# Expert tokens fetched by indirect DMA from a DRAM copy, the residual rows as accumulator, the gate row multiplied in on POOL

## What is computed

```
x = x + gate1 * m                                     # attention half, before the change's place
h = rms_norm(x, g_ffn) * (1.0 + scale2) + shift2
# expert_choice_ffn, for each set (512 latent tokens: cap 64; 128 context tokens: cap 16)
aff = softmax(h @ w_router)                           # 16 experts
gates, idx = top_k(swapaxes(aff, 1, 2), cap)          # each expert picks its cap tokens
xe = h[idx]
ye = (silu(xe @ w_gate) * (xe @ w_up)) @ w_down * gates
x = x + gate2 * zeros.at[idx].add(ye)                 # gate2: one row of 1024 for each set
y = rms_norm(x, g_final)
```

## Time and profile before

| | us |
|---|---|
| median of 3 runs | 1370.84 (1369.69 to 1372.06) |
| profiled execution | 1370.9 |
| its span in the profile | 1368.9 |
| PE / DVE / ACT / POOL busy | 1227.7 / 970.9 / 751.7 / 135.6 |
| first matmul of the first expert group | 702.55 |
| last matmul of the last expert's down product starts | 1323.79 |

### The profile page before, as it was taken

How to read it: one execution, slowest core, us unless ns; L and a number is a source line. 1 busy time by engine, 2 the same in 40 slices (tenths; PEclk the granted TensorE clock), 3 DMA queues, 4 the chain that set the end, 5 groups by cost and what they waited for, 6 DMA issues and landing times.

```text
span 1368.9 us, 17500 instructions
## 1 busy us (share of the span) xinstructions
PE 1227.7 (90%) x6001; PEld 969.7 (71%) x6001; DVE 970.9 (71%) x1245; ACT 751.7 (55%) x1049; POOL 135.6 (10%) x210
## 2 busy tenths in 40 slices
PE   2789987897879999999489999999999999999972
PEld 0568766676767777777378888788887888778851
DVE  1743527788847143244779999999999999799956
ACT  1522225666743212222658887688776887578831
POOL 2131430000000000010440001000010000100002
PEclk9899998999999999999789999999999999999986
DMA  9632221101052543554549997899888997999911
GB/s 325 268 140 64 91 69 39 40 21 40 0 201 75 186 123 124 215 202 154 192 153 383 372 365 243 301 385 369 336 271 286 385 364 271 369 340 379 371 40 77
DMA packets 109481, 295.26 MB, mean 216 GB/s; under 512 B 29857, under 2 KB 31602, under 8 KB 108642
## 3 DMA queue, kind: packets, MB, share of 16 engines
q1 hardware_dynamic: 102802, 265.99, 53.8%
q0 software_dynamic: 6032, 19.43, 4.4%
q10 hardware_dynamic: 576, 8.91, 1.7%
HBM read 276.78 MB, written 12.27 MB: 211 GB/s over the span
## 4 chain that ended last, share of the span: by engine, by line
PE 77%; DVE 11%; DMA 4%; ACT 3%; issue 3%; POOL 1%; SPq 1%; DVEq 0%; ACTq 0%; POOLq 0%
PE ps L1080 12%; PE ps L1081 12%; PE ps L1082 12%; PE ps L671 9%; PE ps L672 9%; PE ps L673 9%; PE ps L849 2%; PE ps L865 2%; DMA raw<-in_w_mod_dram 2%; DVE neg_max L1685 2%; DVE raw_lo L1775 2%; DMA raw<-in_w_exp_up_dram 1%; PE ps L888 1%; PE ps L693 1%; PE ps L1051 1%
## 5 line engine op out<-in xcount | busy, mean ns | idle before, releaser
L1775 DVE TENSOR_TENSOR raw_lo<-raw,w_hi 128x1024 fp32r<-128x1024 f32 x256 | 300.8, 1217 | 33.7 <-ACT w_hi L1421 27.0
L1421 ACT ACTIVATE w_hi<-raw 128x1024 fp32r<-128x1024 f32 x252 | 259.1, 1057 | 62.4 <-PE ps L1082 58.4
L1080 PE MATMUL ps<-w_hi,xe_hi 128*128 128x512 f32 x512 | 207.4, 405 | 1.8 <-DVE xe_lo L1949 1.8
L1082 PE MATMUL ps<-w_hi,xe_lo 128*128 128x512 f32 x512 | 201.7, 394 | 0.0
L1421 ACT ACTIVATE w_hi<-extra 128x1024 fp32r<-128x1024 f32 x128 | 135.7, 1063 | 51.4 <-PE ps L1082 42.2
L1775 DVE TENSOR_TENSOR extra_lo<-extra,w_hi 128x1024 fp32r<-128x1024 f32 x128 | 151.9, 1218 | 10.5 <-ACT w_hi L1421 10.3
L671 PE MATMUL ps<-w_hi,ht_hi 128*128 128x512 f32 (+1 forms) x360 | 142.0, 394 | 12.3 <-DVE raw_lo L494 6.4
L672 PE MATMUL ps<-raw_lo,ht_hi 128*128 128x512 f32 (+1 forms) x360 | 139.3, 387 | 0.0
L673 PE MATMUL ps<-w_hi,ht_lo 128*128 128x512 f32 (+1 forms) x360 | 139.2, 387 | 0.0
L494 DVE TENSOR_TENSOR raw_lo<-raw,w_hi 128x1024 fp32r<-128x1024 f32 x50 | 59.8, 1222 | 99.7 <-ACT w_hi L489 99.3
L489 ACT ACTIVATE w_hi<-raw 128x1024 fp32r<-128x1024 f32 x50 | 50.7, 1054 | 134.9 <-DMA raw<-in_w_in_dram 54.3
(11 more groups left out here) (300 smaller groups left out, 2182.0 us busy)
## 6 DMA issues: line engine op xcount, KB each, us to landing
raw<-in_w_exp_down_dram SPq DMA_DIRECT2D x112, 512.0 KB, 5.3
raw<-in_w_exp_gate_dram SPq DMA_DIRECT2D x80, 512.0 KB, 5.8
extra<-in_w_exp_up_dram SPq DMA_DIRECT2D x64, 512.0 KB, 5.5
raw<-in_w_exp_up_dram SPq DMA_DIRECT2D x64, 512.0 KB, 6.3
raw<-in_w_mod_dram SPq DMA_DIRECT2D x24, 1024.0 KB, 8.6
extra<-in_w_exp_gate_dram SPq DMA_DIRECT2D x48, 512.0 KB, 5.6
raw<-in_w_in_dram SPq DMA_DIRECT2D x17, 1024.0 KB, 5.4
extra<-in_w_exp_down_dram SPq DMA_DIRECT2D x16, 512.0 KB, 5.1
```

The costliest lines, as they stand in the source:

```text
L1080: pe.matmul(b, stat_hi, hi[:, cols], start=(k == 0), stop=False)
L1082: mm = pe.matmul(b, stat_lo, hi[:, cols], start=False, stop=(k == KD - 1))
L1421: act.activation(w_hi[:, (DENSE_SPLITS + h) % NHL, :], expert_half(h), ACT.Copy)\
L1775: dve.tensor_tensor(expert_lo_half(h), expert_half(h), w_hi[:, (DENSE_SPLITS + h) % NHL, :].bitcast(F32), ALU.subtract).then_inc(s_lo, 1)
```

## The change

- **Fetch.** The normalised rows are written once to DRAM (`xn_dram`). For each group PE multiplies the one-hot matrices with `aff_n`, which has a 17th column holding the token number (`find_rows`, 10 float32 matmuls of 17 columns): the result holds for each slot its token number and its gate values. DVE copies them out (`rows_of_group`), POOL fetches the rows by three indirect DMAs (`fetch`: 2 x 128 rows and 64 rows of 4 KB) and waits for them, and PE turns them (16 + 8 transposes). The next group's `find_rows` stands ahead of block d1, POOL's fetch between the outputs of experts 0 and 1. `xn_hi`, `xn_lo`, the DRAM copies of `pos` and `aff` and their spread are gone; `select_slots` compares an iota with the slot's token number.
- **Outputs.** ACT writes `y_g` = PSUM x gate value for all 128 rows (`output_gated`); POOL multiplies by the `gate2` row; ACT, three halves later, makes `ye_hi` and `yc_f` from it; POOL makes `ye_lo`. For the last expert DVE does POOL's part. PE's next down product waits for `output_gated` alone. `gate2` is kept so that each 64-row half holds latent and context row as the expert parity needs; its four spreading matmuls become two of half height each.
- **Accumulator.** `acc` is `x_r` itself, so `finish` is one instruction a tile; the copies of `x_r` and `gate2` to DRAM and back, and the clearing of `acc`, are gone. Combines start three halves later (half 8 in place of 5).

```diff
-        acc = at("acc", 40960, [P, NT, D])
+        acc = x_r
...
+                    if n < 6:
+                        mm = pe.matmul(bank(6), tab2[:, o:o + P], row_of(n), start=True, stop=True)
+                    else:
+                        for half in range(2):
+                            rows = slice(64 * half, 64 * half + 64)
+                            o = T_SB - T_KEPT + (half + event[2]) % 2 * P
+                            mm = pe.matmul(bank(6, rows=rows), tab2[:, o:o + 64], row_of(n), start=True, stop=True)
...
+            def find_rows(n):
+
+                pe.wait_ge(s_ids, 1)
+                pe.wait_ge(s_selg, n * NTL + NTL)
+                pe.wait_ge(s_selc, 3 * n + 3)
+                w = NE + 1
+                for q in range(2):
+                    for t in range(NTL):
+                        pe.matmul(bank(6, q * w, q * w + w), sel_g[:, t, q * P:(q + 1) * P], aff_n[:, t, :],
+                                  start=(t == 0), stop=(t == NTL - 1))
+                pe.matmul(bank(6, 2 * w, 3 * w), sel_w[:, :], aff_n[:, NTL, :], start=True, stop=True)
+                pe.matmul(bank(6, 3 * w, 4 * w, slice(0, EG * CAPC)), sel_c[:, :], aff_n[:, NTL, :],
+                          start=True, stop=True).then_inc(s_slots, 1)
...
             def gather_context(n):
 
-                pe.wait_ge(s_selc, n + 1)
-                pe.wait_ge(s_xl, NT)
                 for k in range(KD):
-                    b = bank(0, k * EG * CAPC, (k + 1) * EG * CAPC)
-                    pe.matmul(b, xn_hi[:, NTL, k * P:(k + 1) * P], sel_c[:, :], start=True, stop=False)
-                    mm = pe.matmul(b, xn_lo[:, NTL, k * P:(k + 1) * P], sel_c[:, :], start=False, stop=True)
+                    mm = pe.transpose(bank(0, k * EG * CAPC, (k + 1) * EG * CAPC), x_gc[:, k * P:(k + 1) * P],
+                                      ident[0:EG * CAPC, 0:EG * CAPC])
                 mm.then_inc(s_gc, 1)
...
                 if k == 0:
-                    pe.wait_ge(s_selg, n * NTL + NTL)
+                    pe.wait_ge(s_xg, 32 * n + 32)
+                    pe.wait_ge(s_xgc, 16 * n + 16)
                 if k == 3:
                     pe.wait_ge(s_xct, 2 * n + 1)
                 if k >= 4:
                     pe.wait_ge(s_xel, n * KD + k - 3)
-                b = bank((k + 1) % 4, 0, EG * CAPL)
-                for t in range(NTL):
-                    pe.matmul(b, xn_hi[:, t, k * P:(k + 1) * P], sel_g[:, t, :], start=(t == 0), stop=False)
-                    mm = pe.matmul(b, xn_lo[:, t, k * P:(k + 1) * P], sel_g[:, t, :],
-                                   start=False, stop=(t == NTL - 1))
+                for q in range(2):
+                    mm = pe.transpose(bank((k + 1) % 4, q * P, (q + 1) * P), x_g[:, q, k * P:(k + 1) * P], ident)
                 mm.then_inc(s_g, 1)
...
+                    if (kind, e) == ("d", 1) and not last:
+                        pe.wait_ge(s_h2l, i * 8 + 4)
+                        find_rows(i + 1)
+                    if kind == "g" and e == EG - 1 and not last:
+                        pe.wait_ge(s_rows, 3 * i + 6)
...
+                def output_gated(e):
+
+                    act.wait_ge(s_half, i * GH + H0 + (AT["d", e] + KD if e >= 0 else 0))
+                    act.wait_ge(s_gep, 8 * i + (8 if e >= 0 else 0))
+                    if not (first and e == 0):
+                        act.wait_ge(s_yel, i * EG + e)
+                        act.wait_ge(s_yec, i * EG + e + 1)
+                    act.activation(y_g[:, :], ps[:, 4 * 512:6 * 512], ACT.Identity, scale=gate_e[:, e % EG:e % EG + 1])\
+                       .then_inc(s_y1, 1)
...
+                    act.wait_ge(s_yg, i * EG + e + 1)
                     if first and e == 0:
                         act.wait_ge(s_yec, 1)
                     e %= EG
                     lat = slice(64 * (e % 2), 64 * (e % 2) + 64)
                     ctx_rows = slice(CROW[e], CROW[e] + CAPC)
-                    act.activation(yc_f[ctx_rows, :], ps[ctx_rows, 4 * 512:6 * 512], ACT.Identity,
-                                   scale=gate_e[ctx_rows, e:e + 1]).then_inc(s_yec, 1)
-                    act.activation(ye_hi[lat, e // 2, :], ps[lat, 4 * 512:6 * 512], ACT.Identity,
-                                   scale=gate_e[lat, e:e + 1]).then_inc(s_yeh, 1)
+                    act.activation(ye_hi[lat, e // 2, :], y_g[lat, :], ACT.Copy).then_inc(s_yeh, 1)
+                    act.activation(yc_f[ctx_rows, :], y_g[ctx_rows, :], ACT.Copy).then_inc(s_yec, 1)
...
+            def rows_of_group(n):
+
+                w = NE + 1
+                dve.wait_ge(s_slots, n + 1)
+                both = bank(6, 0, 3 * w).rearrange("p (q c) -> p q c", c=w)
+                dve.tensor_copy(row_lat[:, :], both[:, 0:2, NE]).then_inc(s_rows, 1)
+                dve.tensor_copy(row_ctx[:, :], bank(6, 4 * w - 1, 4 * w, slice(0, EG * CAPC))).then_inc(s_rows, 1)
+                dve.tensor_copy(slot_n[:, :, :], both).then_inc(s_rows, 1)
...
+                    dve.scalar_tensor_tensor(y_g[:, :], ps[:, 4 * 512:6 * 512], gate_e[:, e:e + 1], gate2[:, e % 2, :],
+                                             ALU.mult, ALU.mult).then_inc(s_yg, 1)
...
             def finish(t):
 
-                if t < NT:
-                    dve.wait_ge(s_add, (NG - 1) * 2 * NT + 2 * t + 3)
-                    if t == 0:
-                        dve.wait_ge(s_fin, 48)
-                    dve.tensor_tensor(acc[:, t, :], acc[:, t, :], gate2_f[:, t // NTL, :], ALU.mult).then_inc(s_fg, 1)
-                    dve.wait_ge(s_fg, t + 1)
-                    dve.tensor_tensor(x_f[:, t, :], x_f[:, t, :], acc[:, t, :], ALU.add).then_inc(s_fx, 1)
-                if t:
-                    dve.wait_ge(s_frs, t)
-                    dve.scalar_tensor_tensor(x_f[:, t - 1, :], x_f[:, t - 1, :], rs[:, t - 1:t], g_fin[:, :],
-                                             ALU.mult, ALU.mult).then_inc(s_fy, 1)
+                dve.wait_ge(s_frs, t + 1)
+                if t == 0:
+                    dve.wait_ge(s_fin, 16)
+                dve.scalar_tensor_tensor(acc[:, t, :], acc[:, t, :], rs[:, t:t + 1], g_fin[:, :], ALU.mult, ALU.mult)\
+                   .then_inc(s_fy, 1)
...
+            def fetch(n, first):
+                pool.wait_ge(s_rows, 3 * n + 3)
+                if not first:
+                    pool.wait_ge(s_g, n * KD)
+                    pool.wait_ge(s_gc, n)
+                for q in range(2):
+                    pool.indirect_dma_start(x_g[:, q, :], None, xn_dram[:, :],
+                                            bass.IndirectOffsetOnAxis(ap=row_lat[:, q:q + 1], axis=0)).then_inc(s_xg, 16)
+                pool.indirect_dma_start(x_gc[:, :], None, xn_dram[:, :],
+                                        bass.IndirectOffsetOnAxis(ap=row_ctx[:, 0:1], axis=0)).then_inc(s_xgc, 16)
+                pool.wait_ge(s_xg, 32 * n + 32)
+                pool.wait_ge(s_xgc, 16 * n + 16)
...
+                def output(e):
+
+                    pool.wait_ge(s_y1, i * EG + e + 1)
+                    pool.tensor_tensor(y_g[:, :], y_g[:, :], gate2[:, e % 2, :], ALU.mult).then_inc(s_yg, 1)
+                    pool.wait_ge(s_yeh, i * EG + e + 1)
+                    e %= EG
+                    rows = slice(64 * (e % 2), 64 * (e % 2) + 64)
+                    pool.tensor_tensor(ye_lo[rows, e // 2, :], y_g[rows, :], ye_hi[rows, e // 2, :].bitcast(F32),
+                                       ALU.subtract).then_inc(s_yel, 1)
+
+                if not first:
+                    output(-1)
+                output(0)
+                if not last:
+                    fetch(i + 1, False)
+                output(1)
+                output(2)
```

More of the change, by code:

```diff
@@ L1055, in combine @@
                 mm.then_inc(s_cmb, 1)
+            find_rows(0)
+            for k in range(3):
+                gather(0, k)
             gather_context(0)
-            for k in range(KD):
+            for k in range(3, KD):
                 gather(0, k)
@@ L1424, in _ @@
             act.wait_ge(s_clear, 1)
+            for k in range(3):
+                gathered(0, k)
             gathered_context(0)
-            for k in range(KD):
+            for k in range(3, KD):
                 gathered(0, k)
@@ L1468, in body @@
                         if before == "d" and k == 1 and (n or not first):
+                            output_gated(e1)
+                        if before == "d" and k == 4 and (n or not first):
                             output_hi(e1)
@@ L1873, in _ @@
             dve.memset(ones16[:, :], 1.0).then_inc(s_dve, 1)
-            dve.wait_ge(s_dve, own())
+            dve.memset(sel_w[:, :], 0.0).then_inc(s_dve, 1)
+            dve.wait_ge(s_dve, own(2))
             dve.wait_ge(s_lgt, 2)
@@ L2047, in body @@
                             expert_lo(h + LEAD, i)
-                        if before == "d" and k == 3 and (n or not first):
-                            output_lo(e1)
```

(9 more changed lines are left out.)

193 lines of the change are left out of this document (75 added, 118 removed).

## The result

The changed kernel takes 1409.13 us (median of 4 runs, 1406.21 to 1414.78) against 1370.86: 1.029 times the time before (95% interval 1.026 to 1.031). It is slower, as forecast, but by 38 us where 9 were forecast, and outside the range.

The account below looks back on a forecast made before the run. PE was taken to bound the groups, with DVE deciding at the experts' start, block d3 and the end. Terms 12.1 + 0.4 - 0.9 + 8.3 - 10.9 = +9.0 gave about 1380.0 us; own range 1374 to 1388, with rivals 1367 to 1392.

Parts of the forecast that it names:

- The sign: Whole kernel: slower by +9.0 us in sum; chances slower 0.71, same 0.16, faster 0.13.
- Startup: Start of the experts: first product at 711.8 instead of 702.55, +9.3, and low clock behind it, +2.8; together +12.1.
- gate2's spread: Four events of two half matmuls each in place of one full matmul: +0.4, at most +3.4.
- `find_rows` in the groups: Ahead of block d1: twenty records of 0.11, 2.3 us of PE a boundary.
- The fetch in the groups: POOL's indirect fetch between expert outputs: no term in the sum; little if landing stays under an expert's 39 us.
- third rival: Fetch slow or ill placed: landing near 12.2 us holds POOL, outputs behind it, ACT and PE; 1389 to 1392; chance 0.15.
- The boundary without `find_rows`: Block d3 to the next group: next group starts at 848.3, not 850.92, -2.6 a boundary before find_rows.
- POOL beside DVE: POOL's output passes delay DVE's extra_lo, add_outputs and hidden: 0.7 times a full-exclusion replay of 11.8, +8.3.
- The gain at the gather: Boundaries: PE saves 7.0 us, but DVE's weight-half and tile pairs limit it; -0.9 for three, find_rows included.
- The end: After the last product: ten DVE passes go, 12.3 us; give back 1.4; -10.9.
- The rival that the meetings are free: DVE's freed passes and the ring of four halves absorb all POOL time: term 0, 1371.7; chance 0.16.
- The rival that the boundary is PE's: DVE ends before PE in d3, 4.7 us saved three times: 1358.5, chance 0.10; half of it, 1365, 0.03.

Follow-up runs that it names:

- e2: Changed kernel with the fetch moved behind output(1) and find_rows moved from ahead of block d1 to ahead of its fifth half: 1377.6 us.
- e5: e2 with POOL's two passes an output cut to 8 columns of 1024: 1364.83 us.
- e6: e2 with DVE making y_g from PSUM in one pass, in place of ACT's eviction and POOL's multiplication; POOL keeps ye_lo: 1370.44 us.
- e8: e2 with two further DVE passes over each of the five tiles at the end: 1386.35 us.
- e3: Changed kernel with the fetch moved behind output(1) and POOL making each ye_lo twice: 1413.12 us.

## Why the prediction failed, point by point

- **The sign: right, but by luck.** Without what the fetch's place (24.7) and the pause and clock around `find_rows` (10.8) added, which the sum put at nothing, the measured terms come to 0, not to the 9 that was forecast. PE is 3.9 us less busy, and the time rose by 38.
- **Startup, +12.1 forecast, +12.5 measured** (10.9 and 1.6). Here two errors cancel, which is luck: the product came 1.6 us later than forecast, mostly because the last landing took 5.4 us from its issue and not 2.9, a plain store being no measure for an indirect fetch; and the low clock cost 1.6 instead of 2.8, as it rose after eight matmuls, not after fourteen as in the earlier trace rows.
- **gate2's spread, +0.4 forecast:** two halves took 1.08 us (four records) where one matmul took 1.02, and the stage ended no later. Nothing. (Its upper bound of 3.4 doesn't follow either: four events doubled are 4 x 1.02 = 4.1.)
- **`find_rows` in the groups, 2.3 forecast, 5.9 measured each**, 17.7 for three instead of 6.9. The step that failed is "`find_rows` ahead of d1 costs 20 x 0.11 = 2.3": the duration was right (2.3 in e2), but the wait for both parts of `ht_lo` that it brings forward was not costed, nor the clock behind pause and thin matmuls, which the same text had costed for the startup.
- **The fetch in the groups, 0 forecast, +24.7 measured.** This is the main failure. The step is in the third rival: "in a group little if landing stays under an expert's 39". The queue was named there in full, `output(1)`, then ACT's `ye_hi` and its weight halves, then PE. But the deadline was taken from the user of the data, an expert away, when the wait stands in POOL's queue and its deadline is the next instruction's: `y_g` of expert 1 was ready at 803.3, 0.4 us after POOL's last issue ended. Every microsecond of the landing beyond that was a delay; ACT's 9.1 us of waiting became 6.5 of PE's, and the slow clock behind them made it 9.5 in the first group, 7.9 and 7.3 in the others. With the landing of 2.9 us that was supposed it would have been little; it was 10 to 11.
- **The boundary without `find_rows`, -7.8 forecast, and POOL beside DVE, +8.3.** Together +0.5; u3, d3 and the start of groups 1 to 3 measured -4.1 + 0.2 = -3.9, of which -2.9 is the gain in group 3 that no term had. e5, where POOL's passes are next to nothing, parts them: its u3 and d3 of the first three groups are 7.1 us shorter than before the change, near the 7.8, though its last group, which has no gather, gets 1.8 shorter as well. Block by block the changed kernel spends 8.8 us more than e5 in u3, d3 and those starts; by medians the passes cost e2 12.8. So the size of the term, 8.3, lies at the low end of what the runs show, and they don't decide between 0.7 times the replay and the whole of it.
- **POOL beside DVE, who meets whom.** The ratio 0.7 taken from the earlier trace rows was 0.59 in the changed kernel (48.6 of 81.9 us), 0.69 in e2 and 0.31 where POOL only subtracts (e6). Wrong was who meets POOL: in the changed kernel `raw_lo` alone, not `hidden`, `add_outputs` or `extra_lo`; `hidden` can be late only through the weight halves ahead of it. The rule of the Trainium skill weighed there ("SBUF — State Buffer", "Who interferes with whom"), that a VectorE instruction with two SBUF inputs contends with a GpSimd instruction that reads SBUF, the trace agrees with: `raw_lo<-raw,w_hi` takes 2.15 us beside a pass of POOL and 1.217 otherwise. Its distinction by the number of SBUF inputs no run here shows.
- **The gain at the gather: right to stop at DVE.** By the prediction's count seven microseconds of PE's work went at each boundary; u3 and d3 got 1.0 to 1.6 shorter with POOL's passes beside them and 1.4 to 3.3 without (e5), and PE waits 1.8 to 2.3 us for `ht_lo` instead of 1.06.
- **The end, -10.9 forecast, -15.5 measured**: -11.4 in DVE's chain as worked out (e8 puts them back), -4.1 in POOL's closing DRAIN, whose reason is open.
- **The rival that the meetings are free** fell by e3 and e5. **The rival that the boundary is PE's** fell by PE's waits for `h_act` and `ht_lo` in every d3.

Sum by the measured terms: 12.5 + 17.7 + 24.7 - 4.1 + 0.2 - 15.5 = 35.5, what lies between the spans.

## What to carry to other kernels

Ask of a wait what stands next in its own queue and when that is due, not when the data are needed: the same fetch a place later cost block g3 nothing. An engine with 90% free time is not a free place for elementwise work, where it slows the busier engine, here at 0.6 to 0.7 for 1 and near that engine's deadline. Price a step inserted into a dense matmul stream with its pause and with the clock behind it, and put it where the stream already waits or doesn't have to.
